# Two sequence mixers woven between the input projections of a transformer-like kernel, in a new order

## The reference

```python
n = rmsnorm(h, norm_mix_w[i]).astype(w_in.dtype)
proj = n @ w_in[i]
q, k, v, gate_lr, g_out, z, xbc, dt_raw = split_cols(proj)
o_gla = gla_mixer(q, k, v, gate_lr, g_out, ...)     # 4 heads, chunks of 64 tokens
o_ssd = ssd_mixer(z, xbc, dt_raw, ...)              # 8 heads, chunks of 128 tokens
mixed = jnp.concatenate([o_gla, o_ssd], axis=-1)
h = h + mixed @ w_out[i]
...
# gla_mixer, per head: G = cumsum(log_a) in the chunk; q*exp(G), k*exp(-G), k*exp(G_last-G)
att = tril(q_in @ k_in); o = att @ v + q_in @ S_prev; S = exp(G_last)*S + k_end.T @ v
o = rmsnorm(o, norm_w) * silu(g_out)                # norm over the 128 values of a head
# ssd_mixer: xbc = silu(conv4(xbc)+b); dt = softplus(dt+b); a_cum = cumsum(dt*A) in the chunk
L = exp(tril(a_cum[l]-a_cum[s])); y = (C @ B.T * L) @ (X*dt) + exp(a_cum) * (C @ S_prev) + X*D
y = rmsnorm_per_group(y * silu(z)) * norm_w
```

## Time and profile before

| | us |
|---|---|
| median of 3 runs | 2852.82 |
| lowest, highest | 2851.92, 2859.35 |
| the profiled execution | 2860.45 |
| its span | 2858.6 |
| TensorE busy in the span | 2702.9 (95%) |
| VectorE busy | 1838.3 (64%) |
| ScalarE busy | 1052.2 (37%) |
| GpSimd busy | 951.4 (33%) |

### The profile page before, as it was taken

How to read it: one execution, slowest core, us unless ns; L and a number is a source line. 1 busy time by engine, 2 the same in 40 slices (tenths; PEclk the granted TensorE clock), 3 DMA queues, 4 the chain that set the end, 5 groups by cost and what they waited for, 6 DMA issues and landing times.

```text
span 2858.6 us, 36074 instructions
## 1 busy us (share of the span) xinstructions
PE 2702.9 (95%) x13725; PEld 2379.8 (83%) x13725; DVE 1838.3 (64%) x3081; ACT 1052.2 (37%) x1659; POOL 951.4 (33%) x534
## 2 busy tenths in 40 slices
PE   8897899999999999999999998899999989899997
PEld 6664689999999999999999977788887866788886
DVE  5555379998988886888888747480543145581542
ACT  4333233434555553333333343432222345422221
POOL 3211331002444443333333134344443422254442
PEclk9876899999999999999999999999999999999999
DMA  4110223656999998999999732132322221133231
GB/s 149 59 37 15 74 74 106 191 154 222 324 340 349 338 321 277 348 347 341 343 346 347 247 100 70 59 110 90 97 96 80 89 94 54 59 104 96 96 96 52
DMA packets 232986, 485.20 MB, mean 170 GB/s; under 512 B 84832, under 2 KB 132848, under 8 KB 232688
## 3 DMA queue, kind: packets, MB, share of 16 engines
q1 hardware_dynamic: 195952, 348.67, 37.6%
q0 software_dynamic: 36864, 134.23, 13.0%
HBM read 439.83 MB, written 42.86 MB: 169 GB/s over the span
## 4 chain that ended last, share of the span: by engine, by line
PE 81%; DVE 14%; ACT 2%; issue 2%; DMA 1%; SPq 0%; POOL 0%; ACTq 0%; DVEq 0%
PE ps L289 24%; PE ps L290 24%; PE ps L291 24%; PE ps L1377 3%; DVE wl L278 2%; PE ps L2076 1%; DVE ti L1237 1%; DVE ti L1232 1%; PE ps L2161 1%; DVE oh L1323 1%; DVE slot L1335 1%; DVE tv L1235 1%; ACT wh L270 1%; DVE cacc L859 1%; DVE bp L1305 1%
## 5 line engine op out<-in xcount | busy, mean ns | idle before, releaser
L270 ACT ACTIVATE wh<-wraw 128x1024 fp32r<-128x1024 f32 x487 | 513.7, 1059 | 1379.5 <-PE ps L291 1373.3
L289 PE MATMUL ps<-Xh,wh 128*128 128x512 f32 (+1 forms) x2200 | 858.3, 390 | 36.7 <-DVE Xl L484 16.3
L278 POOL TENSOR_TENSOR wl<-wraw,wh 128x1024 fp32r<-128x1024 f32 x231 | 560.3, 2431 | 998.3 <-ACT wh L270 998.3
L290 PE MATMUL ps<-Xl,wh 128*128 128x512 f32 (+1 forms) x2200 | 815.8, 371 | 0.0
L291 PE MATMUL ps<-Xh,wl 128*128 128x512 f32 (+1 forms) x2200 | 812.7, 369 | 0.0
L289 PEld LDWEIGHTS ps<-Xh,wh 128*128 128x128 f32 x2200 | 424.0, 193 | 93.1 <-issue 30.4
L290 PEld LDWEIGHTS ps<-Xl,wh 128*128 128x128 f32 x2200 | 423.7, 193 | 48.9 <-issue 2.6
L291 PEld LDWEIGHTS ps<-Xh,wl 128*128 128x128 f32 x2200 | 421.7, 192 | 49.3
L278 DVE TENSOR_TENSOR wl<-wraw,wh 128x1024 fp32r<-128x1024 f32 x256 | 312.4, 1221 | 140.6 <-ACT wh L270 140.4
L289 PE MATMUL ps<-Hh,wh 128*128 128x384 f32 x1024 | 347.1, 339 | 9.7 <-DVE Hl L1587 9.7
L290 PE MATMUL ps<-Hl,wh 128*128 128x384 f32 x1024 | 345.9, 338 | 0.0
(11 more groups left out here) (299 smaller groups left out, 3375.7 us busy)
## 6 DMA issues: line engine op xcount, KB each, us to landing
wraw<-in_uT SPq DMA_DIRECT2D x128, 512.0 KB, 5.2
wraw<-in_v SPq DMA_DIRECT2D x128, 512.0 KB, 5.5
wraw<-in_up SPq DMA_DIRECT2D x128, 512.0 KB, 3.5
gA_scratch<-gl SPq DMA_DIRECT2D x122, 192.0 KB, 5.4
gl<-gA_scratch SPq DMA_DIRECT2D x122, 192.0 KB, 5.4
gG_scratch<-gbuf SPq DMA_DIRECT2D x64, 256.0 KB, 7.8
lg<-gG_scratch SPq DMA_DIRECT2D x128, 128.0 KB, 5.5
wraw<-in_w_q SPq DMA_DIRECT2D x24, 512.0 KB, 3.5
```

The source lines that it names most:

```text
L270: act.activation(wh[:, n % 4, :], wraw[:, n % 4, :], ACT.Copy).then_inc(s_wh, 1)
L278: pool.tensor_tensor(wl[:, n % 4, :], wraw[:, n % 4, :], wh[:, n % 4, :].bitcast(F32), ALU.subtract).then_inc(s_wl, 1)
L289: pe.matmul(o, ah, bh, start=start, stop=False)
L290: pe.matmul(o, ah, bl, start=False, stop=False)
```

## The change

The 23 tiles of the input projection are the same, in another order: dt and gate, the 6 of xBC (B and C first), q, k (`IN_A`, 11 tiles), v, z, and the output gate last, by tokens (`IN_G`). Both mixers stand between them.

- TensorE (`in_pe`): the turning of dt and of the sums after tile 7, `last_sums_pe` after tile 8 (the sums at the end of each chunk for all partitions, in one small matmul), B and X turned between tiles 8 and 10, SSD's scores before v, SSD's states, GLA's turning and GLA's scores within the v tiles, four pairs of SSD heads around the z tiles, GLA's states after them, and GLA's use by blocks of 128 tokens within the gate tiles.
- The sums of the heads are spread by DMA: the 8 x 512 sums go to DRAM and come back broadcast over the partitions (`acD`, `lt_load`), for heads 0 to 3 at once, for 4 to 7 after the pairs before them. `ce` is made for all heads in two operations.
- A pair of heads writes two halves of one bank; for each chunk both products with `LT` come first, then both with the states (`ssd_pair_pe`). GLA's scores, states and use alternate between the two row halves of the array.
- GLA's result has tokens on the partitions. Its norm is a square on ScalarE, a reduction on VectorE, a root and a reciprocal of 4 values per token (`gla_norm_dve`), and no matmul. The product with the gate is turned back by TensorE (`gla_back_pe`) into chunks 0 to 3 of the output projection's input, whose chunks 4 to 7 therefore come first (`out_pe`).
- The convolution's first product is ScalarE's (`conv_act`), the other three VectorE's. ScalarE scales v and the gate on its way out of PSUM. GpSimd makes none of the `Xl` of the output projection any more.
- Tiles in SBUF are laid over each other (`LT` over `Sg`, `ce` over `gs`, `Xw` over `vt`).

```diff
-IN_A, IN_V, IN_R, IN_Z, W_OUT, W_Q, W_U, W_V = 0, 5, 9, 21, 23, 31, 47, 175
+IN_A, IN_V, IN_Z, IN_G, W_OUT, W_Q, W_U, W_V = 0, 11, 15, 19, 23, 31, 47, 175
...
-    B_INA = lin_banks(5)
-    B_INV = lin_banks(4)
-    B_INR = lin_banks(14)
-    B_OUT = lin_banks(8)
+    B_INA = [0, 1, 2, 3, 4, 0, 1, 2, 3, 0, 1]
+    B_TOK4 = [0, 1, 2, 3]
+    B_OUT = [4, 5, 6, 0, 1, 2, 3, 4]
...
+    CONV = (4, 5, 0, 1, 2, 3)
...
+        sp.wait_ge(s_dt, 12)
+        sp.dma_start(acD, acT).then_inc(s_acd, 16)
+        sp.wait_ge(s_acd, ACD[0])
+        for g in range(2):
+            sp.dma_start(ce[64 * g:64 * g + 64, :, :],
+                         acD[4 * g:4 * g + 4, :].unsqueeze(0).to_broadcast([64, 4, T])).then_inc(s_acd, 16)
+        for h in range(4):
+            lt_load(sp, h)
+        for n in range(11, 19):
+            load_w(sp, n)
+        for m in (2, 3):
+            sp.wait_ge(s_yo, m - 1)
+            sp.wait_ge(s_lt, 8 * m)
+            lt_load(sp, 2 * m)
+            lt_load(sp, 2 * m + 1)
+            load_w(sp, 17 + m)
+        for n in range(21, W_OUT + 4):
             load_w(sp, n)
...
+        pool.wait_ge(s_kp, 2)
+        pool.wait_ge(s_ge, 5)
+        pool.memset(GE[:, :, :], 0.0).then_inc(s_g0, 1)
...
+    def last_sums_pe(pe):
+
+        b = AUX["acl"]
+        pe.wait_ge(s_sd, 2)
+        bank_free(pe, b)
+        pe.matmul(ps[b][:, 0:32], ident[:, 127:128].to_broadcast([128, 128]), act_[:, :, :].rearrange("p c h -> p (c h)"),
+                  start=True, stop=True).then_inc(s_sp, 1)
+        freed[b] = (s_sx, 2)
...
+    def ssd_pair_pe(pe, m):
+
+        b, p = AUX[f"y{m}"], slice(64 * (m // 2), 64 * (m // 2) + 64)
+        pe.wait_ge(s_lm, 2 * m + 2)
+        if m == 0:
+            pe.wait_ge(s_ss2, 5)
+            pe.wait_ge(s_xd, 7)
+            pe.wait_ge(s_cm, 2)
+        bank_free(pe, b)
+        for c in range(4):
+            cs = slice(c * 128, c * 128 + 128)
+            for i in range(2):
+                h, op = 2 * m + i, slice(64 * i, 64 * i + 64)
+                mm = pe.matmul(ps[b][op, cs], Xd[:, c, h * 64:(h + 1) * 64], LT[:, h % 4, cs], start=True, stop=(c == 0))
+            for i in range(2):
+                j, op = (2 * m + i) % 4, slice(64 * i, 64 * i + 64)
+                if c:
+                    mm = pe.matmul(ps[b][op, cs], Ss[p, c, j * 64:(j + 1) * 64], ce[p, j, cs], start=False, stop=True)
+        mm.then_inc(s_yo, 1)
+        freed[b] = (s_yz, m + 1)
...
+    def gla_use_pe(pe, tc):
+
+        b = (AUX[f"u{tc}0"], AUX[f"u{tc}1"])
+        ts = slice(tc * 128, tc * 128 + 128)
+        pe.wait_ge(s_ac, 4)
+        pe.wait_ge(s_g0, 2)
+        pe.wait_ge(s_st, 4 * tc + 2)
+        for q in range(2):
+            bank_free(pe, b[q])
+        for m in range(2):
+            ms = slice(m * 128, m * 128 + 128)
+            for q in range(2):
+                h = 2 * m + q
+                pe.matmul(ps[b[q]][:, ms], GE[:, h, ts], vt[:, tc, h * 128:(h + 1) * 128], start=True, stop=False)
             for i in range(2):
                 c = 2 * tc + i
...
+                for q in range(2):
+                    p = slice(64 * q, 64 * q + 64)
+                    mm = pe.matmul(ps[b[q]][64 * i:64 * i + 64, ms], qT[p, m, c * 64:(c + 1) * 64], Sg[p, m, c, :],
+                                   start=False, stop=True)
+        mm.then_inc(s_stp, 1)
+        for q in range(2):
+            freed[b[q]] = (s_gr, 4 * tc + 3 + q)
...
+        def within_g(q):
+            gla_use_pe(pe, q)
+            if q == 1:
+                root_wide_pe(pe, "s1", AUX["r1"])
...
+        project(5)
+        project(6)
+        project(7)
+        turn_dt_pe(pe)
+        project(8)
+        last_sums_pe(pe)
+        turn_b_pe(pe)
+        project(9)
+        turn_x_pe(pe, 0)
+        turn_x_pe(pe, 1)
+        project(10)
+        turn_x_pe(pe, 2)
+        turn_x_pe(pe, 3)
+        ssd_scores_pe(pe)
+        pe_linear_tok(pe, IN_V, 0, B_TOK4, XL["in"], lambda tc: (s_inV, tc + 1), each=within_v)
+        ssd_pair_pe(pe, 0)
+        project_z(0)
+        ssd_pair_pe(pe, 1)
+        project_z(1)
+        ssd_pair_pe(pe, 2)
+        project_z(2)
+        ssd_pair_pe(pe, 3)
+        gla_states_pe(pe, 0)
+        gla_states_pe(pe, 1)
+        project_z(3)
+        gla_states_pe(pe, 2)
+        gla_states_pe(pe, 3)
+        root_wide_pe(pe, "s0", AUX["r0"])
+        pe_linear_tok(pe, IN_G, 0, B_TOK4, XL["in"], lambda tc: (s_gz, tc + 1), each=within_g)
...
+        split_hi(act, 7)
+        act.wait_ge(s_dt, 1)
+        act.activation(z, y, ACT.Abs).then_inc(s_dta, 1)
+        act.wait_ge(s_dta, 1)
+        act.activation(z, z, ACT.Exp, scale=-1.0).then_inc(s_dta, 1)
+        act.activation(ea1[:, :], col("alog", 0, 0, 8), ACT.Exp).then_inc(s_dta, 1)
+        conv_act(act, 0)
+        conv_act(act, 1)
+        split_hi(act, 8)
...
+        for i in range(6):
+            silu_act(act, i)
+            if i < 4:
+                conv_act(act, i + 2)
+            if i >= 1 and i <= 3:
+                split_hi(act, 8 + i)
...
+    def gla_norm_dve(dve, tc):
+        dve.wait_ge(s_gq, 3 * tc + 2)
+        dve.tensor_reduce(gss[:, tc, :], gsq[:, tc % 2, :].rearrange("p (h d) -> p h d", d=128), AX.X,
+                          ALU.add).then_inc(s_gr, 1)
+        dve.wait_ge(s_gq, 3 * tc + 3)
+        dve.reciprocal(gss[:, tc, :], gss[:, tc, :]).then_inc(s_gr, 1)
+        dve.wait_ge(s_gr, 4 * tc + 2)
+        for q in range(2):
+            dve.tensor_tensor(vt[:, tc, :].rearrange("p (m q d) -> p q m d", q=2, d=128)[:, q, :, :],
+                              ps[AUX[f"u{tc}{q}"]][:, 0:256].rearrange("p (m d) -> p m d", d=128),
+                              gss[:, tc, 2 * q:2 * q + 2].unsqueeze(2).to_broadcast([128, 2, 128]),
...
+            conv_dve(dve, 2 + m)
+            xbc_dve(dve, 4 + m)
+        conv_dve(dve, 4)
+        conv_dve(dve, 5)
+        bv = ps[AUX["sp"]][:, 0:64].rearrange("p (c k h) -> p c k h", k=2, h=8)
...
+        qk_dve(dve, 0)
...
-        pe_linear(pe, W_OUT, list(range(8)), B_OUT, XL["out"], done, first=(0, 1, 2))
+
+        for n, kc in enumerate((4, 5, 6, 7, 0, 1, 2, 3)):
+            pe.wait_ge(*XL["out"][kc if kc >= 4 else 3])
+            for g in range(3):
+                if n == 0:
+                    pe.wait_ge(s_wl, W_OUT + g + 1)
+                    bank_free(pe, B_OUT[g])
+                s, cs = (W_OUT + g) % 4, slice(kc * 128, kc * 128 + 128)
+                mm = three(pe, ps[B_OUT[g]][:, :], wh[:, s, cs], wl[:, s, cs], Xh[:, kc, :], Xl[:, kc, :], n == 0, n == 7)
+                if n == 7:
+                    mm.then_inc(s_wuse, 1)
+                    freed[B_OUT[g]] = (s_ho, g + 1)
+            if n < 4:
+                gla_back_pe(pe, n)
+        pe_linear(pe, W_OUT, list(range(3, 8)), B_OUT, None, lambda g: (s_ho, g + 1))
...
```

More of the change, by code:

```diff
@@ L362, in pe_linear_tok @@
             mm.then_inc(s_wuse, 1)
-        for tc in range(4):
-            freed[banks[tc]] = done(tc)
+            if q == 3:
+                for tc in range(4):
+                    freed[banks[tc]] = done(tc)
+            if each is not None:
+                each(q)
     def sum_square(act, name, c, src):
@@ new lines, in in_act @@
+        act.activation(eGl[:, :, :], GE[:, 0:2, :].rearrange("p m (c i) -> p m c i", i=64)[:, :, :, 63], ACT.Exp,
+                       scale=1.0 / 16).then_inc(s_ge, 1)
+        split_hi(act, 12)
+        act.wait_ge(s_sp, 2)
+        act.wait_ge(s_sd, 3)
+        for g in range(2):
+            p = slice(64 * g, 64 * g + 64)
+            act.activation(ead[p, :, :], ps[AUX["acl"]][p, 0:32].rearrange("p (c h) -> p c h", h=8)[:, :, 4 * g:4 * g + 4],
+                           ACT.Exp).then_inc(s_sx, 1)
@@ new lines, in in_act @@
+        split_hi(act, 14)
+        for h in range(4):
+            lt_exp_act(act, h)
+        split_hi(act, 15)
+        for k in range(2):
+            act.wait_ge(s_kp, k + 1)
+            if k == 0:
+                act.wait_ge(s_sp, 1)
+                act.wait_ge(s_const, C_MASK)
+            act.activation(kendt[:, 2 * k:2 * k + 2, :], ps[AUX[f"kt{k}"]][:, :].rearrange("p (a t) -> p a t", a=2),
+                           ACT.Copy).then_inc(s_kt, 1)
+        split_hi(act, 16)
+        split_hi(act, 17)
@@ new lines, in in_act @@
+        act.wait_ge(s_wuse, IN_V + 4)
+        act.wait_ge(s_xp, 8)
+        for tc in range(4):
+            act.activation(vt[:, tc, :], ps[tc][:, :], ACT.Copy, scale=RS4[:, tc:tc + 1]).then_inc(s_inV, 1)
+        split_hi(act, 18)
+        lt_exp_act(act, 4)
+        lt_exp_act(act, 5)
+        split_hi(act, 19)
+        z_act(act, 0)
+        lt_exp_act(act, 6)
+        lt_exp_act(act, 7)
+        split_hi(act, 20)
+        z_act(act, 1)
+        split_hi(act, 21)
+        z_act(act, 2)
+        split_hi(act, 22)
@@ new lines, in conv_dve, with qk_dve @@
+    def conv_dve(dve, i):
+        buf, acc = tmpb[:, 2 + i % 2, :], tmpb[:, i % 2, :]
+        dve.wait_ge(s_cs, i + 1)
+        for k in range(1, 4):
```

(29 more changed lines are left out.)

874 lines of the change are left out of this document (385 added, 489 removed).

## The result

The changed kernel takes 2773.07 us (median of four runs, 2771.88 to 2774.3) against 2852.37 us (four runs, 2848.53 to 2859.35): ratio 0.9719, 95% interval 0.97 to 0.9739, 79 us less. 52 us less were forecast (2801). The profiled execution took 2774.13 us with a span of 2772.4, against 2860.45 and 2858.6.

A forecast was written before the change was run, and what follows sets the result against it. Bound by order, not by an engine. Input stage 83.3 + 76.2 + 56 + 15.5 + 3 = 234, output 54: end 288 against 342.2, 54 less; counting what goes, 48; taken 52, so 2801 us. Range: 2769 less 4, to 2838.

The forecast's parts named there:

- step 1: From 45.5 us to TensorE's wait for VectorE's copies before the last sums: about 15 us idle, going on at 83.3.
- step 2: The other 14 projection tiles at 5.44 us: 76.2 us, with weight loads and the later heads' spreads not late.
- steps 3 and 4: Small matmuls between tiles, 56 us, and lower clock on nine tiles after waits or small work, 1.7 each, 15.5 us.
- step 5: One new TensorE wait, at the norm sum s1 right after use(1), for ScalarE's squares: 3 us.
- rival A: TensorE's clock stays up in the input stage, small work 37 and slow tiles 3: 32 us more gained, 2769; chance 0.15.
- the side by side of column halves: In the head pairs, a skill's rule that array tiles run in parallel: two heads cost as one, 9 us more gained.
- the fall at 145: Profile before, GLA's small products: grant 1.00 from 142 to 145, 0.50 from 146 to 148, no idle; cited against rival A.
- Rival B: VectorE and its collisions with GpSimd's splits late in more places: 12 x 2.1 = 25 us, 2826; chance 0.22.
- Step 6: The output projection after the input stage: 54 us against 44 before, so it costs 10.

The follow-up runs named there:

- e2: The changed kernel with the two heads of each pair one after the other instead of side by side; 2783.87 us, ratio to before 0.9768.
- e6: The changed kernel with the heads of each pair one after the other and the whole pair's products made twice; 2802.26 us, one run.
- e4: The changed kernel with the eight 8 x 512 spreading matmuls put back ahead of the first pair, their output unread; 2786.3 us, ratio to before 0.9781.
- e10: The changed kernel with the old form of GLA's use, head by head, run ahead of the new one in each use; 2794.91 us, one run.
- e7: The changed kernel with each pair's products made four times in a row, both heads side by side; 2804.58 us, one run.
- e9: The changed kernel with TensorE made to wait for a later GpSimd split ahead of pairs 1, 2 and 3; 2803.15 us, one run.
- e5: The changed kernel with seven edits to order on TensorE, VectorE and ScalarE, meant to mend the waits; 2753.08 us, ratio to before 0.9649.

## Why the prediction was right in direction and short in size

The forecast put the end of the input stage at 234 us; it is 205.8. By its own terms:

| term | forecast us | trace us |
|---|---|---|
| TensorE goes on after the last sums (step 1) | 83.3 | 84.6 |
| 14 tiles at 5.44 (step 2) | 76.2 | 76.2 |
| small work and slow tiles (steps 3 and 4) | 56 + 15.5 = 71.5 | 38.0, what is left |
| other waits (step 5) | 3 | 4.8 + 1.2 + 0.5 + 0.5 = 7.0 |
| end | 234 | 205.8 |

*Step 1 was right*: 14.9 us for 15, released by VectorE's copies. The walk along VectorE's queue was good to 1.3 us.

*Step 2 was right*: neither the masks of the later heads nor a weight load stands among the waits.

*Steps 3 and 4 failed, in size.* They charged 31.1 us to half clock: 15.5 on tiles, 4 x 1.9 on pairs, 4 x 1.0 on uses, 4 on the rest. A grant of 0.96 over 121.2 us is 4.8 us lost: 26 too much (the mean grant from 45.5 us on was put near 0.85 and is 0.94). And a pair at full clock was put at 3.9 and takes 2.4, a use at 2.4 and takes 1.9: 4 x 1.5 + 4 x 0.5 = 8 too much. The two make 34 of the 33.5 by which 71.5 exceeds 38.0. I had written down both corrections, rival A with 37 + 3 = 40 us for these steps, and the side by side of column halves with 9 us, and weighed them against one row: the fall at 145. That row was true, but I took it as a property of small products. The second row that I read so, 0.50 in SSD's heads from 235, is another thing: a wait of 1.97 us stands ahead of those heads, and the same products leave the grant at 1.00 where none does (e2, e6). The experiments say the fall without idle time belongs to certain products: those with 8 rows (e4) and, as far as e10 and the trace of before show, those of the old use, both of which the change removes. The products of the pairs do not bring it in 9.5 us (e6, e7). What else brings it is idle time: behind the gaps of 4 us in e9 it fell three times out of three, behind one of 1.83 us in six traces of eleven, and in e5, with the same norm sums and no gap, the grant is 1.00 from 150 to 187. The Trainium skill (TensorE: Matmul & The Clock Gate, Why this matters for your kernels) warns of idle gaps; e9 agrees, with 9.3 us for the clock on 12.6 of gaps; e4 and e10 show that it isn't the only way. Its reading, gapless weaving keeps 2.4 GHz, was rival A, at 0.15, and is in the main what happened.

That 2769 was given for A and 2773 measured is in part luck. A's 37 us of small work are not the sum of its own full-clock values, 4 x 3.9 + 4 x 2.4 + 16 = 41, which would give 2773.5. A left out the 8 us by which pairs and uses are shorter still. And it starts from the forecast of 52 us, the middle of 54 and 48, which is 51. Rival B, VectorE late in more places, did not happen: from 85 us to the end of the input stage TensorE waits for VectorE 2.2 us in all.

*Step 5 was right* where it looked (2.96 for 3) and missed the same wait before the first group (1.83), where ScalarE's squares are late too.

*Step 6 was right*: 53.7 for 54. Missed was the table load, with its squares behind it. In the trace of before ScalarE loads no table between 285 and 346 us; now the SiLUs run in the output projection's first tiles, so the table that the query's root needs is loaded after them, on the chain: 1.28 us at 260.48. TensorE's wait there is 3.3 us, and 1.8 in e5.

The forecast lies 28 us above the median, and the input stage alone accounts for 28 (234 to 205.8). That the two agree so well is chance: taking 52 for the 54 of the walk added 2 us to the miss, and the unedited later stages, where 82.7 us at the marker became 79.3, took 3 from it.

## What to carry to other kernels

Before charging half clock to small work, ask of each form whether this trace shows the fall in *that* form and whether the change keeps it: here the grant fell behind idle gaps and in or right behind two forms of product, and removing these paid twice, once for the work and once for the clock. Look for a wait ahead of each fall before it is put down to the products. Put products on column halves by turns as one does on row halves, and count two as one. When a wait is cut, move the work that releases the next one too: one edit gave 4 us at the marker, seven together gave 19.

## What the runs showed of the hardware that I had not expected

- A float32 pass with 8 rows and 512 columns, sixteen in a row, lets the grant fall from 1.00 to 0.50 with TensorE busy the whole time (e4). Behind 4 us of those that hold 64 rows by 128 columns and stream 64 it fell in two cases of four (e10).
- 128-by-64 and 64-by-64 products leave it at 1.00 for 9.5 us, on one column half of the array alone (e6).
- The same wait of 1.83 us ahead of the same products is followed by 0.50 in six traces and by 1.00 in five.
- Two heads on column halves: 2.42 us for what takes 4.76 in turn (e2).
- VectorE's convolution products met two splits of GpSimd in step 1's walk, where I had counted one: three took 4.25 us and six took 6.63, where three undisturbed took 2.28. VectorE's and GpSimd's timelines, after:

```profile
60.21 2.28 DVE L997 SCALAR_TENSOR_TENSOR tmpb<-tmpb,vec 128x511 f32<-128x511 f32 x3
...
72.73 4.25 DVE L997 SCALAR_TENSOR_TENSOR tmpb<-tmpb,vec 128x511 f32<-128x511 f32 x3
...
77.69 6.63 DVE L997 SCALAR_TENSOR_TENSOR tmpb<-tmpb,vec 128x511 f32<-128x511 f32 x6
```

```profile
72.72 2.93 POOL L274 TENSOR_TENSOR wl<-wraw,wh 128x1024 fp32r<-128x1024 f32 x1 [5.25 <-ACT wh L266]
79.58 2.62 POOL L274 TENSOR_TENSOR wl<-wraw,wh 128x1024 fp32r<-128x1024 f32 x1 [3.92 <-ACT wh L266]
```

Together they cost 4.0 us (4.25 + 6.63 - 3 x 2.28). That is 1.9 more than the 2.1 counted; the other terms of step 1 took 0.6 us less than counted, hence the 1.3.
